# Reordering the modulation dot products of a two-layer decoder kernel: gate units third in each block

## What is computed

```python
def modulate(x, shift, scale):
    return x * (1.0 + scale[:, None, :]) + shift[:, None, :]

def post_norm_residual(x, y, gate, weight, g, b):
    return layer_norm(DEEPNORM_ALPHA * x + weight * (1.0 + gate[:, None, :]) * y, g, b)

for l in range(DEPTH):                       # DEPTH = 2
    if l == N_A_LAYERS:                      # layer 1: shared K/V from the x that layer 0 leaves
        kv_mod = (cond @ w_kv_ada + b_kv_ada).reshape(b, 2, d)
        kv = modulate(x, kv_mod[:, 0], kv_mod[:, 1]) @ w_kv_b
    mod = (cond @ w_ada[l] + b_ada[l]).reshape(b, 3 * N_SUB, d)
    h = modulate(x, mod[:, 0], mod[:, 1])
    x = post_norm_residual(x, swiglu(h, w_ffn_in[l, 0], w_ffn_out[l, 0]), mod[:, 2], 0.5, ...)
    h = modulate(x, mod[:, 3], mod[:, 4])
    ...                                      # layer 0: causal softmax attention; layer 1: stick-breaking
    x = post_norm_residual(x, y, mod[:, 5], 1.0, ...)
    h = modulate(x, mod[:, 6], mod[:, 7])
    x = post_norm_residual(x, swiglu(h, w_ffn_in[l, 1], w_ffn_out[l, 1]), mod[:, 8], 0.5, ...)
```

## Time and profile before

| | |
|---|---|
| time, median of three (lowest, highest) | 1004.49 us (1004.19, 1007.28) |
| profiled execution | 1002.73 us, its span on the core 1000.9 us |
| PE busy | 984.7 us (98%) |
| DVE busy | 774.0 us (77%) |
| ACT busy | 492.4 us (49%) |
| DMA | 269.78 MB, mean 270 GB/s over the span |
| dots (L904) | 144, mean 1.219 us |
| TensorE clock granted | full (mean 0.999) |

### The profile page before, as it was taken

The page is one execution under the profiler, slowest core; times in us unless marked ns, Lnnn a source line. Parts: engine busy times, 40 slices in busy tenths (PEclk is TensorE's granted clock), DMA queues, the critical chain, the costliest instruction groups (busy, mean ns, idle before and its releaser), DMA issues.

```text
span 1000.9 us, 11978 instructions
## 1 busy us (share of the span) xinstructions
PE 984.7 (98%) x4554; PEld 806.9 (81%) x4554; DVE 774.0 (77%) x1143; ACT 492.4 (49%) x670; POOL 82.7 (8%) x160
## 2 busy tenths in 40 slices
PE   9999999999999999999999999999999999999996
PEld 6788888778888888888878888888878878888885
DVE  5888998888768987878795787779689896556646
ACT  4555434465566443434475534334468574343432
POOL 0010111100100111111000011111000100000000
PEclk9999999999999999999999999999999999999999
DMA  9999999838562999999746699989726737647611
GB/s 351 408 409 386 369 384 392 312 132 300 211 231 84 351 367 331 315 316 346 265 158 217 204 359 319 313 309 368 296 91 247 279 132 282 208 162 253 232 50 42
DMA packets 74555, 269.78 MB, mean 270 GB/s; under 512 B 8449, under 2 KB 8577, under 8 KB 74498
## 3 DMA queue, kind: packets, MB, share of 16 engines
q1 hardware_dynamic: 50834, 183.92, 50.5%
q0 software_dynamic: 21792, 78.68, 21.5%
q10 hardware_dynamic: 1872, 6.42, 1.7%
HBM read 267.92 MB, written 1.07 MB: 269 GB/s over the span
## 4 chain that ended last, share of the span: by engine, by line
PE 82%; DVE 7%; DMA 4%; issue 3%; ACT 3%; SPq 1%; DVEq 0%; POOL 0%; ACTq 0%; POOLq 0%
PE psum L1348 18%; PE psum L1350 18%; PE psum L1349 18%; PE psum L1409 7%; PE psum L1407 7%; PE psum L1408 7%; PE psum L1446 2%; DMA raw<-in_w_all 1%; DMA gate<-gate_rows 1%; DVE w_lo L871 1%; DVE qT L1070 1%; DMA ada<-in_w_mod 1%; DVE qT L1069 1%; PE psum L1541 1%; PE psum L1370 1%
## 5 line engine op out<-in xcount | busy, mean ns | idle before, releaser
L871 DVE TENSOR_TENSOR w_lo<-raw,w_hi 128x2048 fp32r<-128x2048 f32 x156 | 353.5, 2286 | 44.4 <-ACT w_hi L492 44.3
L1348 PE MATMUL psum<-w_hi,hT_hi 128*128 128x512 f32 x896 | 356.4, 398 | 1.4 <-DVE hT_lo L895 0.7
L1350 PE MATMUL psum<-w_hi,hT_lo 128*128 128x512 f32 x896 | 350.4, 391 | 0.0
L1349 PE MATMUL psum<-w_lo,hT_hi 128*128 128x512 f32 x896 | 349.6, 390 | 0.0
L492 ACT ACTIVATE w_hi<-raw 128x2048 fp32r<-128x2048 f32 x156 | 294.4, 1917 | 8.0 <-DMA raw<-in_w_all 4.5
L1348 PEld LDWEIGHTS psum<-w_hi,hT_hi 128*128 128x128 f32 x896 | 168.4, 188 | 39.0 <-DVE hT_lo L895 3.5
L527 ACT ACTIVATE tmp<-psum 128x256 f32<-128x256 f32 x88 | 33.5, 384 | 335.6 <-PE psum L1350 334.7
L1350 PEld LDWEIGHTS psum<-w_hi,hT_lo 128*128 128x128 f32 x896 | 168.3, 188 | 35.6
L1349 PEld LDWEIGHTS psum<-w_lo,hT_hi 128*128 128x128 f32 x896 | 168.7, 188 | 32.7
L1407 PE MATMUL psum<-w_hi,a_hi 128*128 128x512 f32 x368 | 148.3, 403 | 0.0
L1409 PE MATMUL psum<-w_hi,a_lo 128*128 128x512 f32 x368 | 144.1, 392 | 0.0
(11 more groups left out here) (153 smaller groups left out, 694.4 us busy)
## 6 DMA issues: line engine op xcount, KB each, us to landing
raw<-in_w_all SPq DMA_DIRECT2D x328, 512.0 KB, 6.1
ada<-in_w_mod POOLq DMA_DIRECT2D x80, 512.0 KB, 6.6
qT<-in_w_mod POOLq DMA_DIRECT2D x64, 512.0 KB, 6.2
v_sb<-in_w_mod SPq DMA_DIRECT2D x6, 512.0 KB, 11.8
qT<-in_w_mod SPq DMA_DIRECT2D x6, 512.0 KB, 11.1
g_row<-in_ln_g ACTq DMA_DIRECT2D x6, 512.0 KB, 6.0
b_row<-in_ln_b ACTq DMA_DIRECT2D x6, 512.0 KB, 8.7
gate<-gate_rows POOLq DMA_DIRECT2D x6, 512.0 KB, 6.3
```

Of the source, the lines that this page charges most:

```text
L871: nc.vector.tensor_tensor(lo_of(n), slot_of(n), hi_of(n).bitcast(F32), ALU.subtract)\
L1348: nc.tensor.matmul(dst, s_hi, m_hi, start=start, stop=False)
L1349: nc.tensor.matmul(dst, s_hi, m_lo, start=False, stop=False)
L1350: return nc.tensor.matmul(dst, s_lo, m_hi, start=False, stop=stop)
```

## The change

The order of the units, the rows done in each stage, and the place of two rows change; no dot is added or removed.

- `ORDER`: each block of five or six units now has its gate third, and unit (0, 8) comes before (1, 0). Gate (0, 2) is the third unit of the first FFN instead of the fifth; units (0, 7) and (0, 5) are the ones with two places (rows 48 to 63). Gate (1, 5) is done in the third FFN, with four places, instead of attention 2.
- Dots per stage: first FFN 37 (before 40), first norm 2 (before 0), projections and softmax of attention 1 nine (before 8), second FFN 40 as before, but six a step from step 3, third FFN 48 (before 40), attention 2 none (before 8), fourth FFN 8.
- GpSimd spreads a gate in the middle of the next unit's loads, not ahead of them.
- `sp_t` lies in `g_row`, the buffer of the norm's weights, not in `gate`. So the wait of gate 4 for the eighth head goes, the first two sums wait for `x_scaled`, and the load of norm 4's weights moves from head 6 to after the last head.

```diff
-ORDER = [(0, 0), (0, 1), (0, 3), (0, 4), (0, 6), (0, 7), (0, 2), (0, 5),
-         (KV, 0), (KV, 1), (1, 0), (1, 1), (0, 8),
-         (1, 3), (1, 4), (1, 6), (1, 7), (1, 2), (1, 5), (1, 8)]
+ORDER = [(0, 0), (0, 1), (0, 3), (0, 4), (0, 2), (0, 6), (0, 7), (0, 5),
+         (KV, 0), (KV, 1), (0, 8), (1, 0), (1, 1),
+         (1, 3), (1, 4), (1, 2), (1, 6), (1, 7), (1, 5), (1, 8)]
...
+ROWS_PER_STEP = [[0] * (OPEN + 1) + [6, 6, 6, 5, 5], [0, 4, 4] + [6] * 7, [0, 4] + [6] * 8, [0] * 6 + [4, 4, 0, 0]]
...
-            p = row % (2 if u in (GATE_OF[1], GATE_OF[4]) else 4)
+            p = row % (2 if u in TWO_PLACE_UNITS else 4)
...
-        sp_t = gate[:, 0:768].rearrange("p (j t) -> p j t", j=2)
+        sp_t = g_row[:, 0:768].rearrange("p (j t) -> p j t", j=2)
...
                 for row in range(8):
+                    if u - 1 in GATE_OF and row == (2 if u in FREED_BY else 4):
+                        spread_gate(GATE_OF.index(u - 1))
...
-                if g == 4:
-
-                    pool.wait_ge(stick_ready, HEADS)
...
-                if h == 6:
+                if h == HEADS + 1:
                     load_ln_rows(4)
...
-                next_dots(40)
+                if f == 3:
+                    next_dots(8, stop)
...
                 dve.wait_ge(gate_in, 16 * i + 16)
+                if i == 0:
+                    next_dots(1, ROWS_BY_QKV)
                 residual(i, 0, 0)
...
                 h_tile(h, 0)
+                if i == 0:
+                    next_dots(1, ROWS_BY_QKV)
                 residual(i, 1, 1)
...
             soft_max(3)
+            next_dots(1, stop)
             soft_scale(3)
-            dot(gate_unit, (6, 7))
-            gate_column(1)
+            next_dots(2, stop)
```

More of the change, by code:

```diff
@@ L905, in dot, with next_dots @@
                                                    op1=ALU.mult, accum_out=modT[:, u, r:r + 1]).then_inc(dots, 1)
+            rows_given = [8 * unit(0, 3)]
+            def next_dots(count, stop):
+                for _ in range(min(count, stop - rows_given[0])):
+                    u, row = divmod(rows_given[0], 8)
+                    dot(u, (row,))
+                    rows_given[0] += 1
+                    if row == 7 and u in GATE_OF:
+                        gate_column(GATE_OF.index(u))
             def gate_column(i):
@@ L947, in ffn @@
             def ffn(f, operands, norm_before=None):
-                n, i, first_unit = N_FFN[f], NORM_OF_FFN[f], FIRST_UNIT[f]
-                given = [0]
-                def next_dots(count):
-                    units = [] if first_unit is None else list(range(first_unit, first_unit + 4))
-                    units.append(GATE_OF[i])
-                    for _ in range(count):
-                        at = given[0]
-                        if at == 8 * len(units):
-                            return
-                        dot(units[at // 8], (at % 8,))
-                        given[0] += 1
-                        if given[0] == 8 * len(units):
-                            gate_column(i)
+                n, stop = N_FFN[f], ROWS_BY_FFN[f]
                 if f == 0:
@@ L1005, in ffn @@
                         x_scaled(norm_before, 1)
-                    if first_unit is not None:
-                        next_dots(2)
+                    if f < 3:
+                        next_dots(2, stop)
                     split_lo(n + 4)
                 for s in range(OPEN + 1 if f == 0 else 1, STEPS - 1):
-                    quarter = 0 if first_unit is None and s < 6 else 3 if f == 0 or s > 6 else 2
+                    rows = ROWS_PER_STEP[f][s]
                     split_lo(n + 3 * s + 2)
@@ L1014, in ffn @@
                         x_shifted(norm_before, s - 2)
-                    next_dots(quarter)
+                    next_dots((rows + 1) // 2, stop)
                     inner_lo(f, s - 1, 1)
@@ L1019, in ffn @@
                     inner_lo(f, s, 0)
-                    next_dots(quarter)
+                    next_dots(rows // 2, stop)
                     split_lo(n + 3 * s + 4)
@@ L1220, in _ @@
             split_lo(n + 5)
-            dot(gate_unit, (0, 1))
+            next_dots(2, stop)
             rope(k0, 1)
@@ L1225, in _ @@
             rope(q1, 0)
-            dot(gate_unit, (2, 3))
+            next_dots(2, stop)
             split_lo(n + 8)
@@ L1237, in _ @@
             rope(k1, 1)
-            dot(gate_unit, (4, 5))
+            next_dots(2, stop)
             soft_max(2)
@@ L1295, in _ @@
             norm(3)
-            n, gate_unit = N_Q, GATE_OF[4]
+            n = N_Q
             split_lo(n + 2)
-            dot(gate_unit, (0, 1))
             split_lo(n + 3)
@@ L1307, in stick_sums @@
                 dve.wait_ge(ln1p_done, h + 1)
-                if h >= 2:
+                if h < 2:
+                    dve.wait_ge(x_scaled_done, 2 * 3 + 2)
+                else:
                     dve.wait_ge(stick_ready, h - 1)
@@ L1323, in _ @@
                     keep_yT(1, h - 3)
-                if h == 1:
-                    dot(gate_unit, (2, 3))
                 if h == 2:
```

27 lines of the change are left out of this document (11 added, 16 removed).

## The result

The changed kernel takes 1006.63 us in the median of 20 runs (1004.72 to 1015.04), the kernel before 1004.62 us (1002.48 to 1009.67, 20 runs); the ratio is 1.0028, 95% interval 1.0014 to 1.0041. Against the 1004.49 us of the first three runs of before it is +2.1 us where +1.3 were predicted, and the time lies in the range.

A forecast was written before the change was run, and what follows sets the result against it. TensorE (PE), busy 984.7 of 1000.9 us, was taken as the bound. Terms of -1.3, -0.4 and +3.0 summed to +1.3 us; on the median of 1004.49 this gave 1005.8 us, range 1002.6 to 1010.5.

The forecast's parts named there:

- Norm 4, -1.3 us: Norm 4: with gate (1, 5) complete before attention 2, the residual starts 1.4 us earlier, of which PE gives back 1.30.
- Norm 0, -0.4 us: First norm: early gate gives -2.0 us, second new dot costs 1.15, and inner(10, 0) 0.4 us late through loads.
- the wait at 190: PE's 1.35 us wait before the last turn_inner of the first FFN, predicted to go.
- my list of what would prove me wrong: No PE wait at head 4, PE waiting for w_lo in step 10, or PE idle in later FFNs' six-dot steps.
- 0.3 us of reserve: First FFN, behind row 50: the split_lo chunk was predicted at 178.5, in time for PE's need at 178.8.
- Attention 1, +3.0 us: Row 63 waits for row 61's place, load 4.9 us; PE stands 2.7 us before head 4 and 0.3 before head 5.
- The rest, at nothing: Six-dot FFN steps, attention 2, norm 4's weight loads, gate writes and read-backs, and two earlier dots: no cost or gain.
- the zero for GpSimd's queue: Gates' writes and read-backs move into FFNs at no cost; loads queued behind them are wanted a slot or more later.
- Slow loads: Rival: loads as slow as in the congested stretch, from 6 us a load; +7.7 us, 1012.2 us; chance 0.15.
- The places don't bind: Rival: all four PE waits go and VectorE's stalls stay covered; 999.7 us; chance 0.05.
- The six-dot steps: Rival: seven on end put VectorE 1 us later each; some 2 us in each of two FFNs; 1009.8 us; chance 0.07.
- the gate was not last: Rival: the wait belongs to something else, so norm 4 gives nothing; +2.6, 1007.1 us; chance 0.05.

The follow-up runs named there:

- before_chain: Kernel before, with dot 5 of gate (0, 5) moved from the first pair to between soft_max(3) and soft_scale(3); 1007.73 us, ratio 1.0013.
- after: The changed kernel itself, first 20 runs and first profile, against the kernel before; 1006.63 us, ratio 1.0028.
- after_again: The changed kernel run once more with no edit, for a second profile; 1009.72 us, ratio to the kernel before 1.0036.
- row63_late: Changed kernel with row 63 and its gate column moved behind the last soft_scale; 1002.31 us, ratio to the kernel before 0.9978.
- busy_wait: Changed kernel with 30 bf16 products of zeros on TensorE before head 4's transposes; 1006.85 us, ratio to the kernel before 1.0013.
- spread_first: Changed kernel with each gate's two spreading DMAs ahead of all eight loads of the next unit; 1031.76 us, ratio to the kernel before 1.026.
- no_norm_dots: Changed kernel with 39 dots in the first FFN, none in norm 0, four places up to row 54; 1005.13 us, ratio to the kernel before 1.0000.
- four_places: Changed kernel with rows 48 to 52 in four places and only rows 53 to 63 in two; 1005.49 us, ratio to the kernel before 0.9996.

## Why the prediction was right, and where its sum was not

**Norm 4, -1.3 us: right.** -1.4 us in every kernel that has it, with the residual behind `split_lo` and no wait for the gate. What the old place costs is less fixed than the sum takes it: in before_chain, which has it too, VectorE waited 2.48 us for the gate there and TensorE 2.44, so against that profile the early gate gives 2.5 us.

**Norm 0, -0.4 us: near in the first profile, in part by luck, and not in the others.** Row 50 waited 4.77 us ("some 4 us"), `inner(10, 0)` came at 184.83 (predicted 184.9), the two transposes waited 1.34 and 1.12 us (predicted 1.3 and 1.5), and the wait at 190 went. The stage gave -0.6 us. But the steps met there by two errors that cancel: row 50's load took 5.6 us, not 4.9, and row 52's took 3.5, not 4.9, so row 52 did not wait at all. The residual came at 195.53, not 194.7: TensorE, and so the silu, was 1.2 us late by step 10, 0.5 us from ahead of 176 and 0.7 from the wait for `w_lo` (0.34 us of it idle in the row, the rest in the distance of the starts). That wait was on my list of what would prove me wrong, and it came in every profile with row 50 in two places: 0.34, 1.64, 1.72, 3.86 and 5.10 us (after, after_again, row63_late, busy_wait, spread_first). The 0.3 us of reserve that I had worked out is less than the load varies by. Of the four of these in which GpSimd's queue is that of the changed kernel, the stage gave -0.6, +0.7, +0.8 and +4.5 us, so -0.4 is its good end and not its middle. No_norm_dots gives the price of the two dots: 1.9 us back between 190 and 210 against the changed kernel. It also shows why they are there: the two rows have to be done somewhere, and in the first FFN the loads are late.

**Attention 1, +3.0 us: the mechanism right, the size wrong.** This is the term that I called most trusted. It was +5.5 us in one profile and +7.9 in the other. The step that failed is the size of the wait and what follows it. I had worked out "so PE stands 2.7 us, and 0.3 more". Two things were missing. The load took 5.9 us and not 4.9; 5.9 was the median of the stage's own row, and I argued it down because fewer transfers lay beside it. In the five profiles of the changed stage it took 5.9, 7.5, 5.6, 5.2 and 4.4 us (after, after_again, busy_wait, four_places, no_norm_dots), so 4.9 was on the low side. That is 1.0 us in the first profile. And the sum stops at the end of the wait, as if TensorE went on as before. It went on at 1.2 GHz: about 1.5 us more, by busy_wait. 3.0 + 1.0 + 1.5 = 5.5. Even the short load of 4.4 us cost 4.2 us, where the sum without the clock would say 2.5. Row63_late shows that the whole term hangs on that one dot: without it, 0.0.

The Trainium skill (TensorE: Matmul & The Clock Gate, HAM oscillation — how this bites in real kernels) describes this for a kernel whose waits for data let the clock fall, so that the work after each wait starts at the lower level. The profile agrees, with one single wait of 3.5 us in a kernel whose TensorE is busy 98% of the time.

**The rest, at nothing: right for the changed kernel.** The six-dot steps of the second and third FFN hold TensorE at 100%; the first stretch is the second FFN's six-dot steps, the second the third's, the last attention 2, which answers to the earlier trace rows:

```profile
330.00:390.00 60.00, 60.00 (x273) 49.43 (x272) 56.06 (x66) 25.89 (x29) 9.49 (x18) 1.00 0.95 355
...
560.00:640.00 80.00, 80.00 (x362) 65.92 (x361) 69.91 (x85) 34.05 (x35) 13.19 (x25) 1.00 0.92 340
...
750.00:799.00 49.00, 48.90 (x267) 42.00 (x266) 34.55 (x54) 37.50 (x61) 0.00 (x0) 1.00 0.42 148
```

But the zero for GpSimd's queue was right by luck: the changed kernel had the spread in a place that works, and I had given no price to either place. In the new order the move is worth 25 us (spread_first).

**The rivals.** Slow loads (1012.2 us, from 6 us a load) is what a part of the runs shows: after_again had 6.0 us waits in both places, a load of 7.5 us, and 1011.22 us in its profiled execution. There it came about otherwise than priced: +7.9 in attention, where 5.8 was the price, and +0.7 in norm 0, where it was 3.15. Of the 20 first runs, 15 lie at 1004.7 to 1007.8 us with a mean clock of 0.995 to 0.997, and five at 1010.5 to 1015.0 with 0.992 to 0.994. That these are runs with a slower load, and a longer stretch of low clock behind it, is inferred from two profiles, not shown for each. "The places don't bind" fell: in the first FFN they cost little (four_places), in attention 1 5.5 us. The six-dot steps fell by the stretches above, and "the gate was not last" by norm 4's -1.4 us.

**The total** came nearer than its parts, and that is luck. The sum was worked out on the profile, where it gave 1004.0 us; the profiled execution took 1006.75, 2.75 us more: 2.5 from attention, 0.5 from ahead of 176, less 0.2 from norm 0 and 0.1 from norm 4. The median (1006.63 for 1005.8) hides this because before's median lies 1.9 us above its profile and the changed kernel's lies 0.1 below its own. Both medians hold runs in which loads were faster or slower than in either profile. Before_chain's profile shows two places where the old order is sometimes slower than in before's: 2.02 us at 191 for 1.35, and 2.44 in norm 4 for 1.30. How much of the 1.9 us comes from there the runs don't show.

## What to carry to other kernels

When a wait is put on TensorE, the price is the wait plus what TensorE does slowly behind it: here 2.3 us of waiting cost 4.2, 3.5 cost 5.5, 5.2 cost 7.9 (0.4 of each would have been the next head's wait), and 5.8 cost 8.6. A reuse of a buffer one dot after it is freed puts a full load on the queue of the engine that reads it; look at what stands behind that instruction, and put it behind the last thing that TensorE needs, since one dot moved behind the softmax of two heads was worth 4.3 us or more. And when a consumer moves earlier, read the issuing engine's queue: two DMAs ahead of eight loads, the first waiting for the last dot of its unit and the second for the first to land, cost 25 us once those loads were wanted at once.
